# Expert stage of a one-layer backbone: 1 MB chunks of whole rows, eight slots that the low part shares with the raw data, and gate, down of the neighbour, up as the order

## The reference, cut to what matters

```python
def expert_choice_ffn(h, w_router, w_gate, w_up, w_down):
    bsz, n, dm = h.shape
    cap = CAPACITY_FACTOR * n // N_EXPERTS
    aff = jax.nn.softmax((h @ w_router).astype(jnp.float32), axis=-1)
    gate, idx = lax.top_k(jnp.swapaxes(aff, 1, 2), cap)
    xg = jax.vmap(lambda hb, ib: hb[ib])(h, idx)
    hid = jax.nn.silu(jnp.einsum('becd,edf->becf', xg, w_gate)) * jnp.einsum('becd,edf->becf', xg, w_up)
    y = jnp.einsum('becf,efd->becd', hid, w_down) * gate[..., None].astype(h.dtype)
    return jax.vmap(lambda yb, ib: jnp.zeros((n, dm), yb.dtype).at[ib.reshape(-1)].add(yb.reshape(-1, dm)))(y, idx)
```

## Time and profile before

| | |
|---|---|
| Runs | 2017.86, 2019.88, 2019.24 us |
| Span of the profiled execution | 2016.1 us, first to last instruction (its own time outside the span is not recorded; the runs lie 1.8 to 3.8 us above the span) |
| Busy | PE 1666.1 us (83%), DVE 1511.7 (75%), ACT 1173.8 (58%), POOL 424.4 (21%) |
| Moved | 512.03 MB, mean 254 GB/s over the span |
| Chain that ended last | PE 59%, DVE 24%, ACT 7%, issue 6%, DMA 2% |

### The profile page before, as it was taken

The page is one execution under the profiler, slowest core; times in us unless marked ns, Lnnn a source line. Parts: engine busy times, 40 slices in busy tenths (PEclk is TensorE's granted clock), DMA queues, the critical chain, the costliest instruction groups (busy, mean ns, idle before and its releaser), DMA issues.

```text
span 2016.1 us, 22336 instructions
## 1 busy us (share of the span) xinstructions
PE 1666.1 (83%) x7413; PEld 1328.0 (66%) x7413; DVE 1511.7 (75%) x1033; ACT 1173.8 (58%) x1104; POOL 424.4 (21%) x277
## 2 busy tenths in 40 slices
PE   7987777778199607898898898898998998998992
PEld 1765556667188506787787787787777777777772
DVE  3688888888822394787887887887787787878874
ACT  4655555556212404766766766766766766667763
POOL 0777777763500220000000000000000000000000
PEclk9998888889599758999999999999999999999996
DMA  9223333323366524999999999999999999999995
GB/s 328 65 63 99 105 99 94 94 68 126 97 196 192 190 92 157 332 374 340 338 376 323 333 361 340 337 355 331 347 363 320 344 363 317 342 362 335 349 324 188
DMA packets 247932, 512.03 MB, mean 254 GB/s; under 512 B 11306, under 2 KB 57048, under 8 KB 247904
## 3 DMA queue, kind: packets, MB, share of 16 engines
q1 hardware_dynamic: 240160, 484.39, 67.6%
q0 software_dynamic: 7744, 27.28, 4.7%
HBM read 480.16 MB, written 31.47 MB: 254 GB/s over the span
## 4 chain that ended last, share of the span: by engine, by line
PE 59%; DVE 24%; ACT 7%; issue 6%; DMA 2%; SPq 2%; ACTq 0%; DVEq 0%; POOL 0%; POOLq 0%
PE psum L1231 12%; PE psum L1232 12%; PE psum L1233 12%; PE psum L1257 5%; PE psum L1259 4%; PE psum L1258 4%; DVE part_l L995 4%; ACT xgT L717 2%; DVE t_bwd L896 2%; DVE t_fwd L896 2%; PE psum L1167 2%; PE psum L1168 2%; PE psum L1169 2%; ACT part_h L552 1%; PE psum L1241 1%
## 5 line engine op out<-in xcount | busy, mean ns | idle before, releaser
L995 DVE TENSOR_TENSOR part_l<-raw,part_h 128x2048 fp32r<-128x2048 f32 x378 | 843.3, 2286 | 85.4 <-ACT part_h L552 85.4
L552 ACT ACTIVATE part_h<-raw 128x2048 fp32r<-128x2048 f32 x384 | 700.7, 1909 | 0.0
L1231 PE MATMUL psum<-part_h,xgT_h 128*128 128x512 f32 x1024 | 416.8, 407 | 73.0 <-DVE part_l L995 68.4
L1232 PE MATMUL psum<-part_h,xgT_l 128*128 128x512 f32 x1024 | 407.5, 398 | 0.0
L1233 PE MATMUL psum<-part_l,xgT_h 128*128 128x512 f32 x1024 | 406.7, 397 | 0.0
L1231 PEld LDWEIGHTS psum<-part_h,xgT_h 128*128 128x128 f32 x1024 | 197.5, 193 | 125.6 <-DVE part_l L995 81.1
L523 POOL COPY id_scatter<-tok_id 128x1 int32 (+1 forms) x16 | 2.9, 181 | 1146.3 <-DVE y_out L1015 1146.3
L552 ACT ACTIVATE hidT_h<-psum 128x512 fp32r<-128x512 f32 x64 | 38.3, 599 | 344.4 <-PE psum L1241 344.4
L1233 PEld LDWEIGHTS psum<-part_l,xgT_h 128*128 128x128 f32 x1024 | 197.5, 193 | 43.4
L1232 PEld LDWEIGHTS psum<-part_h,xgT_l 128*128 128x128 f32 x1024 | 198.1, 193 | 39.6
L1257 PE MATMUL psum<-part_h,hidT_h 128*128 128x512 f32 x512 | 205.9, 402 | 14.3 <-DVE hidT_l L1006 14.3
(11 more groups left out here) (190 smaller groups left out, 2309.9 us busy)
## 6 DMA issues: line engine op xcount, KB each, us to landing
raw<-in_exp_w_gate_dram SPq DMA_DIRECT2D x128, 1024.0 KB, 7.2
raw<-in_exp_w_up_dram SPq DMA_DIRECT2D x128, 1024.0 KB, 7.3
raw<-in_exp_w_down_dram SPq DMA_DIRECT2D x128, 1024.0 KB, 6.6
ada_piece<-in_ada_w_dram SPq DMA_DIRECT2D x64, 256.0 KB, 2.7
win_raw<-in_a_w_in_dram SPq DMA_DIRECT2D x20, 512.0 KB, 5.0
ada_buf<-in_ada_w_dram SPq DMA_DIRECT2D x4, 2048.0 KB, 18.3
y_scr<-y_h POOLq DMA_DIRECT2D x10, 512.0 KB, 3.0
y_scr<-y_l POOLq DMA_DIRECT2D x10, 512.0 KB, 3.2
```

Source lines behind the costliest of these rows:

```text
L552: return nc.scalar.activation(dst, src, ACT.Identity)
L995: v.tensor_tensor(part_l[slot][:], raw[slot][:], part_h[slot][:].bitcast(F32), ALU.subtract).then_inc(sem["part_l_ready"], 1)
L1231: mm(dst, xgT_h[:, kk, :], wh[:, k, :], start=(kk == 0), stop=False)
L1232: mm(dst, xgT_l[:, kk, :], wh[:, k, :], start=False, stop=False)
```

## The change

The expert stage is written anew. What it does:

- A chunk is one block of 128 whole rows of gate or up (8 KB runs), or 256 rows of down as two per partition (8 KB runs). There are 8 chunks for each of gate, down and up, and still 12 matmuls of 512 columns for a chunk.
- There are eight slots of 16 KB. `raw` and `part_l` of a slot lie at the same address, so DVE subtracts in place, and SP may load into a slot only when PE has used the chunk eight earlier (`chunk_used`). ACT and DVE no longer wait for a free slot.
- The order on PE is 8 gate chunks of expert e, 8 down chunks of expert e-1, 8 up chunks of expert e. Gate fills PSUM banks 0 to 3, up banks 4 to 7 (in the order 6, 7, 4, 5 in a chunk), down banks 4 and 5. The hidden transposes of e-1 stand behind gate chunks 1 and 2 of e, and the transposes of the rows of e+1 behind up chunk 3.
- PE waits for `part_h` and `part_l` of a chunk apart, with its high-part products first. The two transposed-row tiles `xgT_h` and `xgT_l` are doubled.
- `hid` is one tile of all 2048 columns. ACT applies SiLU after down chunk 4's copy (when all of gate is done), DVE multiplies after gate chunk 4 of the next expert (when all of up is done), four instructions each.
- Before the stage: the first three chunks are loaded as early as the first six were, five more when the output projection is done; POOL subtracts eight instead of six. `gate2_row`, `router` and `rows3` move up in memory, and their load waits for the last gate products of the mixer.

```diff
--- before
+++ after
-    gate2_row = place("gate2_row", [P, D], F32, 84)
+    gate2_row = place("gate2_row", [P, D], F32, 128)
...
-    NS = 6
-    part_h = [place(f"part_h{s}", [P, 4 * HALF], F32R, 16 * s) for s in range(NS)]
-    part_l = [place(f"part_l{s}", [P, 4 * HALF], F32R, 16 * s + 8) for s in range(NS)]
-    raw = [place(f"raw{s}", [P, 4 * HALF], F32, 96 + 8 * s) for s in range(NS)]
-    xg = place("xg", [P, D], F32, 146)
-    xgT = place("xgT", [P, KD, P], F32, 150)
-    xgT_h = place("xgT_h", [P, KD, P], F32R, 154)
-    xgT_l = place("xgT_l", [P, KD, P], F32R, 158)
-    act_g = [place(f"act_g{s}", [P, HALF], F32, 162 + 2 * s) for s in range(2)]
-    hid = [place(f"hid{s}", [P, HALF], F32, 176 + 2 * s) for s in range(2)]
-    hidT_h = [place(f"hidT_h{s}", [P, 4, P], F32R, 180 + 4 * s) for s in range(2)]
-    hidT_l = [place(f"hidT_l{s}", [P, 4, P], F32R, 182 + 4 * s) for s in range(2)]
-    y_out = place("y_out", [P, D], F32, 188)
+    NS = 8
+    part_h = [place(f"part_h{s}", [P, FF], F32R, 16 * s) for s in range(NS)]
+    part_l = [place(f"part_l{s}", [P, FF], F32R, 16 * s + 8) for s in range(NS)]
+    raw = [place(f"raw{s}", [P, FF], F32, 16 * s + 8) for s in range(NS)]
+    xg = place("xg", [P, D], F32, 128)
+    xgT = place("xgT", [P, KD, P], F32, 132)
+    xgT_h = [place(f"xgT_h{s}", [P, KD, P], F32R, 136 + 4 * s) for s in range(2)]
+    xgT_l = [place(f"xgT_l{s}", [P, KD, P], F32R, 144 + 4 * s) for s in range(2)]
+    hid = place("hid", [P, FF], F32, 152)
+    hidT_h = place("hidT_h", [P, FF // P, P], F32R, 160)
+    hidT_l = place("hidT_l", [P, FF // P, P], F32R, 168)
+    y_out = place("y_out", [P, D], F32, 176)
...
-    wg_v = exp_w_gate[0].rearrange("e (k p) f -> e p k f", p=P)
-    wu_v = exp_w_up[0].rearrange("e (k p) f -> e p k f", p=P)
-    wd_v = exp_w_down[0].rearrange("e (k p) f -> e p k f", p=P)
+    wg_v = exp_w_gate[0].rearrange("e (k p) f -> e k p f", p=P)
+    wu_v = exp_w_up[0].rearrange("e (k p) f -> e k p f", p=P)
+    wd_v = exp_w_down[0].rearrange("e (k p r) f -> e k p (r f)", p=P, r=2)
...
+    CHUNKS = 8
+    group_of = lambda e, kind: {"g": 3 * e - 1, "d": 3 * E - 1 if isinstance(e, int) and e == E - 1 else 3 * e + 3, "u": 3 * e + 1}[kind]
+    first_group = {"g": 0, "u": 1}
+    def chunk(e, kind, i, first=False):
+        group = first_group[kind] if first else group_of(e, kind)
+        return group * CHUNKS + i
+    slot_of = lambda i: (i + 5) % NS
+    EARLY = NS
...
-            sp.wait_ge(sem["wo_l_dve"], 1)
+            sp.wait_ge(sem["gate_done"], 12 * NB)
...
-                if not first:
-                    sp.wait_ge(sem["part_h_ready"], e * CH + i - NS - 1)
-                    sp.wait_ge(sem["part_l_ready"], e * CH + i - NS - 1)
-                sp.dma_start(dst, src.rearrange("o p k f -> (o p) k f")).then_inc(raw_loaded[slot], 16)
+            def load_chunk(e, kind, i, first=False):
+                src = {"g": wg_v, "u": wu_v, "d": wd_v}[kind]
+                slot = slot_of(i)
+                c = chunk(e, kind, i, first)
+                if not (first and kind == "g"):
+                    sp.wait_ge(sem["chunk_used"], c - NS + 1)
...
-            for i in range(2, 2 + NS):
-                load_chunk(0, i, first=True)
+            for i in range(3):
+                load_chunk(0, "g", i, first=True)
...
+            sp.wait_ge(sem["proj_done"], 2 * NT)
+            for i in range(3, CHUNKS):
+                load_chunk(0, "g", i, first=True)
...
+                for i in range(CHUNKS):
+                    load_chunk(e, "g", i)
+                for i in range(CHUNKS):
+                    load_chunk(e - 1, "d", i)
+                for i in range(CHUNKS):
+                    load_chunk(e, "u", i)
+            for i in range(CHUNKS):
+                load_chunk(E - 1, "d", i)
...
+            for i in range(EARLY):
+                slot = slot_of(i)
+                pool.wait_ge(sem["part_h_ready"], i + 1)
...
+            def gated(e, first=False):
+                act.wait_ge(sem["chunk_used"], chunk(e, "g", CHUNKS - 1, first) + 1)
...
+                for f in range(NF):
+                    nc.scalar.activation(hid[:, f * HALF:(f + 1) * HALF], bank(f), ACT.Silu).then_inc(sem["silu_done"], 1)
...
+            def expert(e, slot):
+                for i in range(CHUNKS):
+                    split(e, "g", i)
+                    if i == 0:
+                        gathered_rows(e, slot)
+                    if i == 6:
+                        turn_hidden(e - 1)
+                for i in range(CHUNKS):
+                    split(e - 1, "d", i)
+                    if i == 4:
+                        gated(e)
+                for i in range(CHUNKS):
+                    split(e, "u", i)
...
+            def gate_up(e, first=False):
+                dve.wait_ge(sem["silu_done"], e * NF + NF)
+                dve.wait_ge(sem["chunk_used"], chunk(e, "u", CHUNKS - 1, first) + 1)
+                for f in range(NF):
+                    cols = slice(f * HALF, (f + 1) * HALF)
+                    v.tensor_tensor(hid[:, cols], hid[:, cols], bank(4 + f), ALU.mult).then_inc(sem["hid_ready"], 1)
...
+            def expert(e, slot, before_first=False):
+                for i in range(CHUNKS):
+                    split(e, "g", i)
+                    if i == 1:
+                        gathered_rows(e, slot)
+                    if i == 4:
+                        gate_up(e - 1, before_first)
+                    if i == 7:
+                        turn_hidden(e - 1)
+                for i in range(CHUNKS):
+                    split(e - 1, "d", i)
+                for i in range(CHUNKS):
+                    split(e, "u", i)
+                    if i == 4:
                         expert_out(e - 1)
...
+            def in_product(e, kind, i, slot, first=False):
+                c = chunk(e, kind, i, first)
+                wh, wl = weights(slot_of(i), NF)
+                xh, xl = xgT_h[slot][:, i, :], xgT_l[slot][:, i, :]
+                banks = [(f, bank(f)) for f in range(NF)] if kind == "g" else [(f, bank(4 + f)) for f in (2, 3, 0, 1)]
+                pe.wait_ge(sem["part_h_ready"], c + 1)
+                if kind == "g" and i == 0:
+                    pe.wait_ge(sem["xgT_l_ready"], e + 1)
+                for n, (f, dst) in enumerate(banks):
+                    if kind == "u" and i == 0 and n == 2 and not first:
+                        pe.wait_ge(sem["y_ready"], e * 2)
+                    mm(dst, xh, wh[:, f, :], start=(i == 0), stop=False)
+                for f, dst in banks:
+                    mm(dst, xl, wh[:, f, :], start=False, stop=False)
+                pe.wait_ge(sem["part_l_ready"], c + 1)
+                for f, dst in banks:
+                    last = mm(dst, xh, wl[:, f, :], start=False, stop=(i == CHUNKS - 1))
...
+                    lo = (2 * f + k // 2) * 2 * P + k % 2
+                    last = nc.tensor.transpose(bank(4 + f)[:, k * P:(k + 1) * P], hid[:, lo:lo + 2 * P - 1:2], ident[:])
...
+                pe.wait_ge(sem["part_h_ready"], c + 1)
+                halves = [(n, slice(n * HALF, (n + 1) * HALF)) for n in range(2)]
+                for k in range(2):
+                    hh, hl = hidT_h[:, 2 * i + k, :], hidT_l[:, 2 * i + k, :]
+                    for n, cols in halves:
+                        mm(bank(4 + n), hh, wh[:, k, cols], start=(i == 0 and k == 0), stop=False)
+                    for n, cols in halves:
+                        mm(bank(4 + n), hl, wh[:, k, cols], start=False, stop=False)
...
+            def turn_rows(e):
+                pe.wait_ge(sem["gathered"], e * 16 + 16)
+                if not (isinstance(e, int) and e == 0):
+                    pe.wait_ge(sem["silu_done"], e * NF)
...
+            def expert(e, slot, last=False):
+                for i in range(CHUNKS):
+                    in_product(e, "g", i, slot)
+                    if i in (1, 2):
+                        turn_hidden(e - 1, 2 * i - 2)
+                        turn_hidden(e - 1, 2 * i - 1)
+                downs(e - 1)
+                for i in range(CHUNKS):
+                    in_product(e, "u", i, slot)
+                    if i == 3 and not last:
+                        turn_rows(e + 1)
...
+            for f in range(NF):
+                turn_hidden(E - 1, f)
+            downs(E - 1)
```

More of the change, by code:

```diff
@@ L678, in _, with split @@
             nc.scalar.activation(soft[:, 0:NT, 0:E], soft[:, 0:NT, 0:E], ACT.Exp).then_inc(sem["exp_done"], 1)
[L680 to L686 removed]
+            def split(e, kind, i, first=False):
+                slot = slot_of(i)
+                group = first_group[kind] if first else group_of(e, kind)
+                act.wait_ge(raw_loaded[slot], group * 16 + 16)
@@ L687, in split @@
                 copy(part_h[slot][:], raw[slot][:]).then_inc(sem["part_h_ready"], 1)
             act.wait_ge(sem["gated_done"], 2 * NT)
-            for key in order[2:2 + NS]:
-                split(0, key)
-            def hidden(e, f):
```

(46 more changed lines are left out.)

213 lines of the change are left out of this document (58 added, 155 removed).

## The result

The changed kernel takes **2069.14 us** (median of 4 runs, 2067.93 to 2071.67) beside 2019.56 us for the kernel before (median of 4 runs, 2017.86 to 2021.71). The ratio is 1.0252, with a 95% interval of 1.0235 to 1.0269: 2.5% slower. Forecast were 1975 us and a range of 1945 to 2009. The profiled execution has a span of 2066.2 us (2016.1 before).

The account below looks back on a forecast made before the run. PE was taken to set the pace in the expert stage, with loads also near their limit. Terms -90 + 42 + 18 - 4 - 15 + 4 gave -45 us, forecast 1975 us; 80% range 1945 to 2009.

Parts of the forecast that it names:

- Old pauses: PE's pauses at each expert's turn, including waits for `part_l`, go: 15 turns by 6.0 us, -90 us.
- Pause A: New PE wait for `y_out`, two matmuls behind down chunk 7: 2.8 us by 15, +42 us.
- Pause B: New PE wait for the hidden rows, at the transposes behind gate chunk 1: 1.2 us by 15, +18 us.
- Restarts: Fewer PE restarts after pauses, some three an expert at 0.1 us: -4 us.
- Clock: Most falls of the granted clock in the expert stage should go, leaving 5 of 20 us: -15 us.
- The end: Last expert's down chunks all follow its hidden rows; PE restarts at about 6.2 us, against 1.9 before: +4 us.
- Loads: Expert-stage loads move the same bytes, asking for 362 GB/s in a 72.5 us period: 0 us.
- R2: Rival: late loads behind pause A, landing after 10.5 us, make pause A 8.0 and the time 2068 us; chance 0.07.
- R1: Rival: the expert stage's loads bind at 353 GB/s, period 74.3 us, 1997 us in all; chance 0.19.
- R4: Rival: order doesn't matter as thought; pauses only move and time stays within 4 us of 2019; chance 0.06.
- R3: Rival: pause A makes the clock fall every period, costing about 2.8 us each, 2011 us; chance 0.10.
- signs of being wrong: PE waiting for `part_l` or `part_h` inside a group, landings above 9 us, clock under 0.97, product step above 0.235 us.

Follow-up runs that it names:

- both edits: Changed kernel with POOL's gather ahead of the scatter and DVE writing `y_out` behind up chunk 3's split, not up chunk 4's: 1931.73 us, ratio 0.9574.
- the first run with 2 KB rows: Kernel with gather ahead of scatter and earlier `y_out`, its gate and up loads again 4 row blocks by 512 columns: 1943.55 us, ratio 0.9627.

## Why the prediction was wrong

The step that failed is one that the prediction did not take: **POOL's list**, and with it the gather, which stood in the sum with no term at all. It followed `y_out` to PE ("behind this wait stand all of PE's up products"), but `y_out` has a second reader, the scatter, and behind the scatter stands the gather. The diff moved `y_out` from the start of the turn to the up phase, and moved the use of the gathered rows from the turn to up chunk 3; POOL's own lines were untouched, and so I did not read them. The account ahead of the prediction had the same hole: it says that POOL gathers the rows of the next expert as soon as `xgT_h` is there. In the turn of the earlier trace rows `xgT_h` is there at 1215.87 and the gather is issued at 1231.68, behind `y_out` and the scatter. The trace before had what the sum needs: from the end of `y_out` (1227.93) to the gather's issue (1231.68) 3.75 us, and 6.2 us of landing, are 10.0 us, against 10 matmuls and 3 chunks of PE, 10 x 0.23 + 3 x 2.76 = 10.6 us. A margin of 0.6 us, 14 times over, where the old order had 49. That sum would have shown a thin margin, and not yet a wait of 5.5 us: the rest is growth. In the turn shown the same two pieces took 7.4 and 10.4 us, together 7.9 more than 10.0. Of this, 3.7 are POOL's instructions (`id_scatter` 2.08 instead of 0.18, from the scatter to the next copy 2.26 instead of 1.03, `id_gather` 1.33 instead of 0.76), and the rest is the landing. PE's work took 13.2 instead of 10.6 us, part of it at the lower clock, which hides 2.6 of it.

Point by point, in the prediction's terms:

- *Old pauses, -90 us*: right. No wait for `part_l` is left.
- *Pause A, +42*: right. 35.7 us in 15, 2.4 each where 2.8 were taken. The landing of `raw` has a median of 4.8, near the 5.3 that I chose over the median of the earlier trace rows; where up chunk 4 landed late (6.67 us in the turn shown, next line) the wait was 3.7.

```profile
1014.59 6.67 DMA raw<-in_exp_w_up_dram
```

- *Pause B, +18*: too high. There is no such wait before the end, nor is there in the run with the gather first: 0.
- *The gather, in no term*: +76.6.
- *Restarts, -4*: not measured by itself.
- *Clock, -15*: wrong in sign. Behind pauses of 3.7 and 4.6 us PE runs at the lower clock (0.50 from 1026.9 us on, and 11 of the 14 groups of eight transposes that wait for the gather last 1.95 to 1.97 us, as the last one above, against 1.04 in the earlier trace rows). Of a period of 79.5 us 66.2 + 2.1 are PE's steps, 2.4 pause A, 5.5 the gather; the other 3.3 I put down to the clock, by subtraction, where it was 1.3. That is 14 x 2.0 = +28 instead of -15. With the gather first the same subtraction leaves 1.3 again.
- *The end, +4*: too small. From the last up product to the first down product with the hidden rows are 10.3 us (6.2 forecast, 1.9 before), +8: the hidden rows stand behind the split of down chunk 4, whose copy starts only at 2000.68, where I had its load landed 5.3 us behind up chunk 4, at about 1997.

```profile
1999.18 1.07 PE L1232 MATMUL psum<-part_l,xgT_h 128*128 128x512 f32 x4
2004.83 2.48 DVE L992 TENSOR_TENSOR hid<-hid,psum 128x512 f32<-128x512 f32 x4
...
2010.41 0.72 PE L1252 MATMUL psum<-part_h,hidT_h 128*128 128x512 f32 x2 [1.49 <-DVE hidT_l L997]
```

- *Loads, 0*: right. With most waits cured the stage moves 378 GB/s over 1015 us, and rows of 2 KB do as well.

The sum with the measured terms is -90 + 36 + 77 + 28 - 4 + 8 = +55; the spans differ by 50. The 5 us between them I did not trace; the clock term is a subtraction and takes in what the restarts cost, so -4 and +28 are not apart in the record.

Of the rivals, R2 had named 2068 us, but this is not it: it wanted `raw` to land after 10.5 us and pause A to be 8.0; they were 4.8 and 2.4. That it named the measured time is chance. R1 falls with the 378 GB/s, and so does the ceiling of 358 GB/s from the Trainium skill ("DMA: Bandwidth & Descriptors", "Where 436 GB/s comes from"): this core, alone, stood above it for a whole millisecond. R4 falls, since each cured pause came off the time. R3 was half right: pauses of this length do cost the clock. Of the signs of being wrong, the clock average under 0.97 came (0.95); the others look at the loads, and no sign looked at the gather.

The kernel that the prediction had priced is the one with the gather first: 1966 us, 9 below the forecast of 1975. What the change does to the old pauses and with pause A was as described; one list was missing from it. That this kernel lies so near the forecast is in part luck: neither pause B (+18) nor the gain in clock (-15; its window has 0.98, as before) is there, and the two errors nearly cancel. In the terms above it is -90 + 35 + 0 - 4 + 0 + 8 = -51, a span of 1965, where 1962.7 was measured.

## What to carry to other kernels

When a change moves a write (here `y_out`), list every reader of it on every engine, and for each reader what stands behind it in its own list; an untouched and nearly idle engine can hold the transfer that the critical one needs. When the place of use moves as well, compute the new slack of each transfer that is used there, from the moment its issue is released. What an edit is worth depends on the waits that stand beside it: one split earlier was worth 14 us while the gather hung on `y_out`, and 34 us after.

## What the runs showed of the hardware

**A tiny copy on POOL waits for DVE.** `id_scatter`, 128 integers, took 0.18 us before and 2.08 in the changed kernel. At 1027.01 it starts 0.24 us behind a subtraction of DVE (1026.77, 2.29 us long) and ends at 1029.09, 0.03 us behind that subtraction; it took 2.08 or more in all 15 turns, and 0.18 in the last one, when DVE has no split to make. With DVE idle from 1014.35 to 1019.49 us, `id_gather` takes 0.18 (here the kernel with both edits):

```profile
1012.06 2.29 DVE L989 TENSOR_TENSOR part_l<-raw,part_h 128x2048 fp32r<-128x2048 f32 x1 [0.89 <-ACT part_h L545]
...
1017.88 0.18 POOL L502 COPY id_gather<-tok_id 128x1 int32 x1 [9.64 <-ACT xgT_h L545]
```

The Trainium skill states this: by "SBUF — State Buffer", section "SBUF: two separate sides", a DVE operation with two SBUF inputs and a GpSimd operation that reads SBUF exclude each other for a whole instruction. The trace agrees, 2.08 against 0.18 us. What it costs the kernel was not tried by itself: a kernel that makes this copy ahead of the wait for `y_out` has not been run.

**The clock follows the pauses.** With waits of at most 1.7 us for `y_out` the stage kept 1.00 (both edits); with waits up to 4.7 us at the same place and no other before the end it had 0.98 (gather first); with waits of 1.8 to 4.5 us for `y_out` and of 4.4 to 7.1 us for the gathered rows in nearly every turn it had 0.95. The clock is the likely reason why taking away 76.6 us of waits gave 103 us: what is left of a turn beside steps and waits fell from 3.3 to 1.3 us.

**DMA share and rate are not one number.** 378 GB/s were moved at a share of 0.98 with 8 KB rows, and 379 at 1.02 with 2 KB rows; a share of 1.00 at 370 GB/s, in the first run with 2 KB rows, was not a sign that the loads bind.
